# Order of the 512- and 256-column products within a weight chunk, in a two-block transformer kernel on one core

## The reference

```
def conv_ffn(x, w_up, conv_w, conv_b, w_down):
    h = x @ w_up                      # 2048 -> 2 * 5632
    h = conv over 3 tokens of h, + conv_b
    gate, val = split(h)
    return (silu(gate) * val) @ w_down
```

## Time and profile before

| | |
|---|---|
| median of 3 runs | 3342.15 us (3340.41 to 3346.95) |
| the profiled execution | 3340.91 us |
| its span | 3339.1 us |
| granted TensorE clock, mean | 0.996 |
| busy share of PE, PEld, DVE, ACT, POOL | 99%, 85%, 67%, 41%, 9% |
| DRAM read | 608.36 MB, 183 GB/s with what is written |

### The profile page before, as it was taken

The page is one execution under the profiler, slowest core; times in us unless marked ns, Lnnn a source line. Parts: engine busy times, 40 slices in busy tenths (PEclk is TensorE's granted clock), DMA queues, the critical chain, the costliest instruction groups (busy, mean ns, idle before and its releaser), DMA issues.

```text
span 3339.1 us, 42990 instructions
## 1 busy us (share of the span) xinstructions
PE 3295.3 (99%) x17716; PEld 2829.0 (85%) x17716; DVE 2236.6 (67%) x2217; ACT 1379.6 (41%) x1058; POOL 287.4 (9%) x108
## 2 busy tenths in 40 slices
PE   8999999999999999999999999989999999999999
PEld 7888888888888888888888888878888888888887
DVE  6746677877874465767787784458866566555664
ACT  5534343333333345643333333335733333354433
POOL 1300101111120000000111110000012011000000
PEclk9999999999999999999999999989999999999999
DMA  6554345555555545455555555545555545545554
GB/s 253 204 201 176 126 165 189 189 186 183 186 189 219 197 173 178 138 189 186 184 186 189 189 185 218 190 163 189 184 188 191 193 164 181 189 152 182 198 188 164
DMA packets 88448, 617.27 MB, mean 185 GB/s; under 512 B 10320, under 2 KB 11216, under 8 KB 15312
## 3 DMA queue, kind: packets, MB, share of 16 engines
q1 hardware_dynamic: 83232, 592.34, 49.0%
q10 hardware_dynamic: 5040, 22.35, 2.0%
HBM read 608.36 MB, written 2.10 MB: 183 GB/s over the span
## 4 chain that ended last, share of the span: by engine, by line
PE 95%; DVE 2%; ACT 1%; DVEq 1%; DMA 1%; issue 0%; ACTq 0%; SPq 0%
PE acc L318 39%; PE acc L317 20%; PE acc L372 7%; PE acc L374 7%; PE acc L373 7%; PE acc L314 3%; PE acc L331 2%; PE acc L333 2%; PE acc L332 2%; PE acc L315 1%; PE acc L1711 0%; PE acc L561 0%; DVE w_lo L229 0%; DMA w_raw<-weights_dram 0%; PE acc L1494 0%; PE acc L1492 0%
## 5 line engine op out<-in xcount | busy, mean ns | idle before, releaser
L318 PE MATMUL acc<-x_hi_lo,w_hi 128*128 128x512 f32 x5580 | 1968.7, 397 | 0.0
L229 DVE TENSOR_TENSOR w_lo<-w_raw,w_hi 128x2048 fp32r<-128x2048 f32 x558 | 1351.6, 2424 | 832.8 <-ACT w_hi L225 831.7
L225 ACT ACTIVATE w_hi<-w_raw 128x2048 fp32r<-128x2048 f32 x558 | 1068.5, 1917 | 1598.9 <-PE acc L318 993.9
L317 PE MATMUL acc<-x_hi_lo,w_lo 128*128 128x256 f32 x5580 | 1572.7, 282 | 1.0 <-DVE x_hi_lo L549 1.0
L318 PEld LDWEIGHTS acc<-x_hi_lo,w_hi 128*128 128x128 f32 x5580 | 1048.5, 188 | 248.4 <-issue 0.7
L317 PEld LDWEIGHTS acc<-x_hi_lo,w_lo 128*128 128x128 f32 x5580 | 1054.5, 189 | 8.3 <-issue 2.5
L372 PE MATMUL acc<-w_hi,hidden_hi_lo 128*128 128x512 f32 x832 | 323.7, 389 | 0.0
L373 PE MATMUL acc<-w_lo,hidden_hi_lo 128*128 128x512 f32 x832 | 323.7, 389 | 0.0
L374 PE MATMUL acc<-w_hi,hidden_hi_lo 128*128 128x512 f32 x832 | 323.7, 389 | 0.0
L374 PEld LDWEIGHTS acc<-w_hi,hidden_hi_lo 128*128 128x128 f32 x832 | 156.2, 188 | 32.5
L373 PEld LDWEIGHTS acc<-w_lo,hidden_hi_lo 128*128 128x128 f32 x832 | 156.2, 188 | 32.4
(11 more groups left out here) (265 smaller groups left out, 2321.5 us busy)
## 6 DMA issues: line engine op xcount, KB each, us to landing
w_raw<-weights_dram SPq DMA_DIRECT2D x558, 1024.0 KB, 4.8
over<-rows_dram ACTq DMA_DIRECT2D x10, 1024.0 KB, 8.3
over<-over ACTq DMA_DIRECT2D x20, 128.0 KB, 2.4
u_tiles<-x_dram SPq DMA_DIRECT2D x4, 512.0 KB, 7.8
w_raw<-weights_dram SPq DMA_DIRECT2D x4, 512.0 KB, 6.9
resid<-x_tok_dram ACTq DMA_DIRECT2D x1, 2048.0 KB, 8.6
over<-w_gates_dram ACTq DMA_DIRECT2D x1, 2048.0 KB, 8.1
out_dram<-resid SPq DMA_DIRECT2D x8, 256.0 KB, 2.1
```

The costliest lines, as they stand in the source:

```text
L225: act.activation(whi[:, n % NHI, :], raw[:, n % NRAW, :], ACT.Copy).then_inc(weights_hi, 1)
L229: dve.tensor_tensor(wlo[:, n % NRAW, :], raw[:, n % NRAW, :], whi[:, n % NHI, :].bitcast(F32), ALU.subtract).then_inc(weights_split, 1)
L317: nc.tensor.matmul(*rest, start=False, stop=False)
L318: last = nc.tensor.matmul(*both, start=False, stop=(k == CK * nch - 1))
```

## The change

Within a feature-major chunk the products are put in groups, and in a group all 512-column products are issued first, then all 256-column ones. A group is the whole chunk (16 and 16, by kk, then f, in the last chunk of a task too). In the first task after a norm a group is one k: four and four over f, with `before_k` ahead of each group, in the last chunk as well. In chunks 0 and 1 a group is one (f, kk), in the order of before; there the 512-column product now always comes first. The stop flag sits on the 256-column product of the last k. Counts, shapes, operands, waits at the start of a chunk and the increment at its end are the same. Token-major products are untouched.

```diff
@@ -291,32 +291,27 @@
                         if isinstance(i, int) and (i, t) in by_token:
                             token_chunk(c, n, 4 * t, nch).then_inc(chunk_used, 1)
                             continue
+                        first = before_k and isinstance(i, int) and (i, t) == (0, 0)
+                        tile = lambda f, kk: (f * CK + kk) * P
                         if n < 2:
-                            places = [(2 * h + f, kk) for h in range(2) for kk in range(CK) for f in range(2)]
-                        elif c < nch - 1:
-                            places = [(f, kk) for kk in range(CK) for f in range(CF)]
+                            groups = [[(f, kk)] for h in range(2) for kk in range(CK) for f in (2 * h, 2 * h + 1)]
+                        elif first:
+                            groups = [[(f, kk) for f in range(CF)] for kk in range(CK)]
                         else:
-                            places = [(f, kk) for f in range(CF) for kk in range(CK)]
-                        first = before_k and isinstance(i, int) and (i, t) == (0, 0)
-                        if first and c == nch - 1:
-                            for kk in range(CK):
-                                before_k(CK * c + kk)
-                        for f, kk in places:
-                            bank, k = 4 * t + f, CK * c + kk
-                            if first and c < nch - 1 and f == 0:
-                                before_k(k)
-                            if n < 2 and (f, kk) == (2, 0):
+                            groups = [[(f, kk) for kk in range(CK) for f in range(CF)]]
+                        for group in groups:
+                            if first:
+                                before_k(CK * c + group[0][1])
+                            if n < 2 and group[0] == (2, 0):
                                 pe.wait_ge(weights_split, n + 1)
-                            w0 = (f * CK + kk) * P
-                            both = (acc[:, bank, :], whi[:, n % NHI, w0:w0 + P], moving(k, 0, 2 * T))
-                            rest = (acc[:, bank, 0:T], wlo[:, n % NRAW, w0:w0 + P], moving(k, 0, T))
-                            if k == 0:
-                                nc.tensor.matmul(*both, start=True, stop=False)
-                                last = nc.tensor.matmul(*rest, start=False, stop=False)
-                            else:
-                                nc.tensor.matmul(*rest, start=False, stop=False)
-                                last = nc.tensor.matmul(*both, start=False,
-                                                        stop=(k == CK * nch - 1))
+                            for f, kk in group:
+                                k = CK * c + kk
+                                pe.matmul(acc[:, 4 * t + f, :], whi[:, n % NHI, tile(f, kk):tile(f, kk) + P],
+                                          moving(k, 0, 2 * T), start=(k == 0), stop=False)
+                            for f, kk in group:
+                                k = CK * c + kk
+                                last = pe.matmul(acc[:, 4 * t + f, 0:T], wlo[:, n % NRAW, tile(f, kk):tile(f, kk) + P],
+                                                 moving(k, 0, T), start=False, stop=(k == CK * nch - 1))
                         last.then_inc(chunk_used, 1)
 
         def token_chunk(c, n, bank0, nch):
```

## The result

The changed kernel takes 3321.48 us in the median of 4 runs (3321.39 to 3323.95), the kernel before 3343.82 us beside it (4 runs, 3340.41 to 3346.95): ratio 0.994, 95% interval 0.9928 to 0.9952. The profiled span fell from 3339.1 us to 3319.6, by 19.5. A second measurement of the changed kernel, further down, gave the same ratio.

What follows compares the result with a forecast made beforehand. The prediction took TensorE's rate through its products as the bound. Savings of 22.7 + 3 = 25.7 us off the profiled 3340.91 gave 3315.2, written as 3316 us for the runs' median, range 3275 to 3338.

Steps and rivals of the forecast that it cites:

- The bound: Whole kernel: the rate at which TensorE goes through its products sets the time, covering 3295.3 of 3339.1 us.
- The 256s in a run: Each chunk's sixteen 256-column products in a row: 120 ns each, 1920 ns together.
- Rival A: Runs of 256-column products go quicker than 120 ns, at 113 or 111.6, giving 3271 to 3300 us; chance 0.25.
- C: Rival: weight loads bound the 256s in 362 chunks' second halves, slower from 124 ns each, 3346 us up; chance 0.08.
- lower bound of 111.6 ns: Least time for a 256-column product in a run, from 32 half-length products with own loads in 3.57 us.
- The 512s in a run: Each chunk's sixteen 512-column products in a row: 226.7 ns each, 3627 ns, as in token-major chunks.
- both changes of length: Switches between 512- and 256-column products in a chunk: about 3 ns together.
- The sum: Per chunk 3627 + 1920 + about 3 ns = 5.55 us; 223 chunks save 0.102 each, 22.7 us.
- the other 139 chunks: Chunks in short stretches or beside recurrence and attention work: gain between 0 and 14 us, taken as 3.
- What may be late next: Feeding the shorter chunks: loads, cast and split keep pace, VectorE at 4.5 us a chunk, so TensorE's gain stays undiminished.
- The first tasks: First tasks after a norm, 16 chunks in groups of four and four: gain taken as 0, at most 1.6 us.
- Rival B: Time goes by columns alone, so chunks stay at 5.65 us, 3342 us, or 3330 to 3342 with partial gain; chance 0.15.

Runs made afterwards that it cites:

- the short products: Changed kernel with the w_lo products over 128 columns instead of 256 from chunk 2 on, leaving part of the computation out: 3289.48 us (1 run).
- The last experiment: Changed kernel with the first task after a norm also grouped sixteen and sixteen, all four waits at a chunk's head: 3340.81 us, ratio 0.9997 (10 runs).

## Why the prediction was right, and where it was off

**The bound.** TensorE's succession of products sets the time, and 19.0 of the 19.5 us saved lie in the chunks counted below: right.

**The 256s in a run.** Predicted 120 ns from two neighbours and from 346.7 - 226.7; measured 1.91 us for sixteen and 3.84 us for thirty-two. This step carried the forecast. Rival A (113 ns) fell. C has a floor to point to, but it lies below C's deciding point: it would allow 111 ns, and C decides from 124. The prediction's lower bound of 111.6 ns came from float32 products, and these do not show a bound by loads: float32 products of 256 columns lie (1.89 - 0.38) / 7 = 0.216 us apart in attention, so that 128 columns would by themselves take 108 of the 111.6.

```profile
1293.13 0.38 PE L1329 MATMUL acc<-u_tiles 128*128 128x256 f32 x1
...
1293.13 1.89 PE L1329 MATMUL acc<-u_tiles 128*128 128x256 f32 x8
```

That the bound was nearly right is luck; the run of 128-column fp32r products is what shows it.

**The 512s in a run.** 226.7 once settled. The term that was mis-sized is the opening: I gave both changes of length 3 ns a chunk together, and they cost 20, as the groups of eight, sixteen and thirty-two show. The excess of the first 512 behind a 256 was seen, that of the four that follow it was not.

**The sum.** 5.567 us a chunk in place of 5.55, so 0.085 us saved against 0.102 at each of the 223 counted chunks: 223 x 0.085 = 19.0 us, not 22.7; the casts of the same chunks add up to 18.9. The spans differ by 19.5, so the other 139 chunks and the first tasks brought about 0.5 net and not 3: those at 5.65 gained, those at 5.55 lost 0.02 each. The medians differ by 22.3 us where 26 was forecast from 3342.15 to 3316; the 2.8 us by which they differ more than the spans are scatter between the executions. So both terms of the forecast 25.7 were too large, by 3.7 and 2.5 us; that the difference of the medians comes within 4 us of it is in part this scatter.

**What may be late next.** No new wait on a split, and at 5.567 us a chunk loads, cast and split kept pace: right. Even 437.8 / 80 = 5.473 us a chunk, with the short products, ran through up0 without a wait of TensorE.

**The first tasks.** I costed the groups of four at 0 and did not price the alternative. The last experiment shows that this exception is worth about as much as the rest of the change.

**Rival B.** Its premise, that the 5.65 rate is there whatever the order, is refuted by the changed kernel, where neither half of a chunk shows it. The Trainium skill, "TensorE: Matmul & The Clock Gate", section "Back-to-back issue gap", gives the formula that the prediction weighs for an isolated product, not for a stream of loads and products, and no run here shows a pair at its 325 ns. Within a run the time does follow the columns: 226.7 and 120.0 ns are both the columns at 2.4 GHz plus 13.3 ns. Its doubt was sound in another way: the same alternation at both rates shows that the gain is against a pattern, not against alternation as such.

## What to carry to other kernels

Where products of two lengths alternate, measure pairs from start to start in several stages: a rate above the sum of both lengths' own may be a pattern that grouping by length removes, and here runs of sixteen and of two (one execution) took nearly all of it away, while runs of four and eight gave part of it back. A change of order that moves waits to the head of a group must leave small groups where operands are still arriving. And where a run of equal products has a step at its opening, halve the number of openings by turning every second group.

## What was not expected of the hardware

The same alternating 512- and 256-column products run at 5.55 or at 5.65 us per 16 pairs, and keep the one or the other for as long as 80 chunks; neither a preceding run of 256s nor a float32 product in front selects the shorter one. With strict alternation single executions lay 18 us apart, while the grouped kernel's first four lay within 2.6 us. A run of 512s behind 256s needs about five products to reach 226.7 ns. A run of 128-column products with their own loads comes down to 111 ns each, where their columns are 53.
